# Differential attention: both scores of a tile ahead of its turns, and the low copy between the two exponentials

## What is computed

```python
def one(qblk):                                   # a block of 128 queries
    s = jnp.einsum('bqhsd,bkhsd->bhsqk', qblk, k).astype(jnp.float32) * scale
    p = jax.nn.softmax(s, axis=-1)
    a = p[:, :, 0] - lam * p[:, :, 1]
    return jnp.einsum('bhqk,bkhe->bqhe', a.astype(v.dtype), v)
```

## Time and profile before

| | us |
|---|---|
| median of 3 runs | 1749.78 (1749.14 to 1750.22) |
| profiled execution | 1748.26 |
| its span | 1746.5 |
| TensorE busy | 1702.2 (97%) |
| VectorE busy | 1210.1 (69%) |
| ScalarE busy | 809.1 (46%) |
| POOL busy | 806.2 (46%) |
| mean granted TensorE clock | 0.995 |

### The profile page before, as it was taken

How to read it: one execution, slowest core, us unless ns; L and a number is a source line. 1 busy time by engine, 2 the same in 40 slices (tenths; PEclk the granted TensorE clock), 3 DMA queues, 4 the chain that set the end, 5 groups by cost and what they waited for, 6 DMA issues and landing times. The chain is left out here.

```text
span 1746.5 us, 26024 instructions
## 1 busy us (share of the span) xinstructions
PE 1702.2 (97%) x9248; PEld 1439.5 (82%) x9248; DVE 1210.1 (69%) x1654; ACT 809.1 (46%) x1593; POOL 806.2 (46%) x579
## 2 busy tenths in 40 slices
PE   8999999999998999989999999899999999999998
PEld 7997888888877999879888878678888888878887
DVE  4438688789948999778733466866656655585767
ACT  3435333345637888657611246633333333354453
POOL 1308677776533899445422323455555555300000
PEclk9999999999999999999999999999999999999999
DMA  9333244335677665512054322132333232386734
GB/s 351 99 125 117 97 157 156 146 125 200 254 196 190 172 148 137 156 33 74 2 199 162 123 108 85 66 127 96 108 128 113 96 124 104 120 285 221 248 98 180
DMA packets 98571, 249.90 MB, mean 143 GB/s; under 512 B 12321, under 2 KB 26017, under 8 KB 98338
## 3 DMA queue, kind: packets, MB, share of 16 engines
q1 hardware_dynamic: 98466, 248.52, 42.6%
HBM read 183.07 MB, written 65.41 MB: 142 GB/s over the span
## 5 line engine op out<-in xcount | busy, mean ns | idle before, releaser
L766 POOL TENSOR_TENSOR ring<-raw_w,ring 128x512 fp32r<-128x512 f32 x120 | 187.1, 1579 | 137.3 <-ACT ring L637 137.3
L78 PE MATMUL psum<-h_hi,ring 128*128 128x512 f32 x400 | 155.9, 390 | 2.8 <-ACT z L683 2.0
L79 PE MATMUL psum<-h_lo,ring 128*128 128x512 f32 x400 | 155.6, 389 | 0.0
L80 PE MATMUL psum<-h_hi,ring 128*128 128x512 f32 x400 | 155.6, 389 | 0.0
L78 PE MATMUL psum<-u_slot 128*128 128x512 f32 x308 | 120.4, 391 | 1.3 <-DVE u_slot L2992 1.1
L80 PE MATMUL psum<-u_slot 128*128 128x512 f32 x308 | 120.1, 390 | 0.0
L79 PE MATMUL psum<-u_slot 128*128 128x512 f32 x308 | 119.9, 389 | 0.0
L637 ACT ACTIVATE ring<-raw_w 128x512 fp32r<-128x512 f32 x120 | 72.5, 625 | 102.0 <-DVE raw_w L927 39.3
L1418 DVE TENSOR_REDUCE mx<-psum 128x1 f32<-128x1280 f32 x64 | 95.1, 1487 | 6.7 <-PE psum L1304 6.0
L1351 ACT ACTIVATE e<-psum,neg_m 128x1280 f32<-128x1280 f32 x64 | 85.0, 1328 | 30.6 <-DVE neg_m L1419 30.6
L2591 POOL TENSOR_TENSOR cut_lo<-i_raw,cut_hi 128x512 fp32r<-128x512 f32 x44 | 66.8, 1519 | 59.3 <-ACT cut_hi L2446 59.3
(11 more groups left out here) (424 smaller groups left out, 5171.0 us busy)
## 6 DMA issues: line engine op xcount, KB each, us to landing
raw_w<-in_w_pairs SPq DMA_DIRECT2D x40, 512.0 KB, 4.9
qk_dram<-room SPq DMA_DIRECT2D x26, 512.0 KB, 3.6
room<-in_w_ada SPq DMA_DIRECT2D x24, 512.0 KB, 5.5
gates_dram<-ost SPq DMA_DIRECT2D x24, 512.0 KB, 3.1
b_g<-gates_dram SPq DMA_DIRECT2D x8, 1536.0 KB, 7.7
stage<-in_w_ff SPq DMA_DIRECT2D x22, 512.0 KB, 5.8
i_raw<-in_w_ff SPq DMA_DIRECT2D x22, 512.0 KB, 4.9
f_dram<-h SPq DMA_DIRECT2D x22, 512.0 KB, 3.3
```

The source lines that it names most:

```text
L78: pe.matmul(out, sh, mh, start=first, stop=False, skip_group_check=onto)
L79: pe.matmul(out, sh, ml, start=False, stop=False, skip_group_check=onto)
L80: return pe.matmul(out, sl, mh, start=False, stop=last, skip_group_check=onto)
L766: pool.tensor_tensor(w_lo[i], source(p, i), w_hi[i].bitcast(F32), ALU.subtract).then_inc(w_lo_ready, 1)
```

## The change

On TensorE the second scores of tile i move ahead of the wait for `a` and of the low turns; all ten turns then follow each other. On ScalarE the first exponential of tile i moves ahead of the copy of the low turns, which then stands between the two exponentials. Everything else stays: the same instructions with the same waits.

```diff
@@ -1321,12 +1321,10 @@
                 t = i - LAG_TURN
                 if i < TILES:
                     scores(i, 0)
+                    scores(i, 1)
                 if 0 <= t < TILES:
                     pe.wait_ge(a_ready, t + 3)
                     turn(t, i, "low")
-                if i < TILES:
-                    scores(i, 1)
-                if 0 <= t < TILES:
                     turn(t, i, "high")
                     bank = turn(t, i, "last")
                 elif t >= TILES:
@@ -1390,10 +1388,11 @@
             for s in range(2):
                 act.sem_inc(exp_done[s], 1)
             def step(i):
+                if i < TILES:
+                    exp(i, 0)
                 if LAG_TURN <= i < TILES + LAG_TURN:
                     copy_out(i, "low")
                 if i < TILES:
-                    exp(i, 0)
                     exp(i, 1)
                 if LAG_TURN <= i < TILES + LAG_TURN:
                     copy_out(i, "high")
```

## The result

The changed kernel takes 1803.55 us (median of four runs, 1800.86 to 1806.97), the kernel before beside it 1749.46 us. The ratio is 1.0309, with a 95% interval from 1.0296 to 1.0322: slower by 54 us. The profiled execution of the changed kernel took 1806.97 us, with a span of 1805.2 us.

A forecast was written before the change was run, and what follows sets the result against it. TensorE sets the pace, VectorE close behind. The change closes a six-term loop of 7.61 us a tile over 28 tiles, 52.6 us later, giving 1802.4 us; 4.5 for clock falls makes 1806 us, range 1797 to 1824.

The forecast's parts named there:

- The bound: Differential attention stage: TensorE sets the pace, busy 19.93 of 20 us, VectorE close behind at 18.59; ScalarE has room.
- The loop of 7.61 us: First scores, maximum, first exponential, low copy, last turns, products, next scores: six start-to-start distances, 7.61 us a tile.
- The wait of 1.8 us a tile: TensorE stands some 1.8 us in every tile before the last turns, until ScalarE has copied the low turns out.
- The sum for the stage: Differential attention: 28 tiles of 7.61 us, so the window stage begins at 758.4 instead of 705.83, 52.6 us later.
- The steps after the loop: Steps 32 to 34 of the stage have no exponential and keep their order, so they cost 0.
- The clock: TensorE's stops make its granted clock fall a few times: three falls, +4.5 us, bounds 0 and 14 falls (+21).
- The price of a fall: Each fall of TensorE's granted clock was estimated to cost 1.5 us.
- The rival with many falls: TensorE's clock falls in about every second tile or more: 14 falls of 1.5 us, 1823 us; chance 0.20.
- The rule of the Trainium skill: Short idles between matmul groups cycling through PSUM banks swing TensorE's clock; by it most tiles would have a slow stretch.
- The rival that works: Low copy done before TensorE reaches the last turns, 3.4 us after first scores; no loop, about 1744 us; chance 0.02.
- the saved switch: One switch from turns to scores on TensorE goes: at most 0.08 us a tile, 2.4 us in 30 tiles.

The follow-up runs named there:

- act_half: Kernel before the change with only ScalarE's half: low copy between the two exponentials, TensorE's order as before; 1802.16 us, ratio 1.029.
- low_after_both: Changed kernel with the low copy behind both exponentials instead of between them; 1903.6 us, ratio 1.087.
- both_filled: low_after_both with the four high turns of tiles 0 to 29 done five times over, sixteen transposes more a tile; 1850.96 us, ratio 1.0579.
- high_thrice: Changed kernel with the four high turns of tiles 0 to 29 done three times over, eight transposes more a tile; 1801.82 us, ratio 1.029.
- trim_three: trim_two with the last turns and products of the tiles in the loop put into the emptied bank 5; 1747.38 us, ratio 0.9984.
- trim_two: Changed kernel without the third piece (256 keys) of each tile's second scores, ring still of two banks; 1821.98 us, ratio 1.0412.
- pe_half: Kernel before the change with only TensorE's half: second scores ahead of all ten turns, ScalarE's order as before; 1757.77 us, ratio 1.0038.

## Why the prediction was right

- *The bound.* TensorE set the pace and ScalarE's low copy stood 1.34 us ahead of the first exponential, invisible in the list of waits. Right: act_half moves that copy alone and loses all of it.
- *The loop of 7.61 us.* Right to 0.01 us in each term (7.62 in the tile above); low_after_both and both_filled lengthen it by the term that was added, high_thrice shows that TensorE's turns are not in it, trim_three opens it.
- *The wait of 1.8 us a tile.* 47.3 us in 27 tiles in the list of 545 to 750 us: 1.89 us in the first, 1.73 to 1.76 in the others.
- *The sum for the stage.* Forecast 52.6 us; measured 54.4 us. Two traces have the same loop without a fall of the clock in it, act_half and high_thrice; their stages take 237.5 and 237.4 us, 52.8 us more than the 184.61 of before. So the loop was forecast to 0.2 us, and the other 1.5 us are one fall of the clock: tile 4's first scores come 8.73 us after tile 3's, tile 5's 8.25 us after tile 4's, together 1.76 more than twice 7.61, where the same two tiles of act_half take 0.22 more. The steps after the loop cost nothing, as said.
- *The clock.* The direction was right, the number of falls was guessed: three in the stage, one seen in this trace (the low stretch of 528 to 534 us in the earlier trace rows, before the loop closes, is in both kernels). It came behind the longest wait of the loop; the 28 waits of 1.73 to 1.76 us that followed left the clock at 1.00:

```profile
545.55 0.44 PE L1311 MATMUL psum<-ident,a 128*128 128x128 f32 x2 [1.89 <-ACT at L1356]
545.83 3.46 PE L1317 MATMUL psum<-val,at 128*128 128x128 f32 x20
```

```profile
547.00:550.00 3.00, 3.00 (x14) 2.81 (x14) 0.35 (x2) 0.92 (x4) 0.00 (x0) 0.50 1.10 366
550.00:560.00 10.00, 8.27 (x57) 7.38 (x56) 6.39 (x8) 4.94 (x13) 7.53 (x6) 0.98 0.42 167
550.00:755.00 205.00, 157.86 (x1131) 142.09 (x1130) 142.85 (x189) 124.98 (x271) 136.77 (x106) 1.00 0.46 123
```

  The forecast was 2.5 us above the median, and two falls too many, 3 us, are about that. That it came so near is partly luck: the four runs lie 6 us apart, and the profiled one has 4.3 us outside the stage for which the sum had no term. The price of a fall, 1.5 us, holds: trim_two's stage takes 257.3 us, 20 more than high_thrice's, and the products are slowed down in 13 of its tiles. The rival with many falls was closer than its trace made it look: trim_two, with 0.23 us more of waiting and as much less of work a tile, took 1821.98 us, where that rival had 1823.
- *The rule of the Trainium skill* ("TensorE: Matmul & The Clock Gate", section on psum-queue depth-cycling): the swing of the clock that it tells of is in low_after_both in nearly every tile and in trim_two in every second or third, not in the changed kernel. The pattern was the right one; the idles of the changed kernel, 1.74 us, were just short enough, where 1.97 us in trim_two were not.
- *The rival that works.* Its condition was named wrongly. I wrote that it decides at 3.4 us and that only the exponential stands in the way. pe_half has the exponential out of the way, and the copy still holds the last turns, by 0.25 us, since the low turns come later themselves. And its gain was priced too high: trim_three has the loop open, and of the saved switch, priced at 0.08 us a tile, some 0.02 are left. So the price of the change's benefit was wrong, with no effect on the sum, in which it was hidden.

## What to carry to other kernels

When an instruction is moved behind another in an in-order queue, list what the other one waits for and who waits for the moved one; if the second list leads back to the first, add up the start-to-start distances round the loop and compare the sum with the pace of now. A wait that doesn't show in a profile (here the one of the last turns for the low copy) is only a wait that is covered; a ring of two buffers that is used three times a tile has such a wait in each tile. And where TensorE is made to wait in every tile, look at how near the wait comes to one that drops its clock; work put into the wait, even useless work, can be worth more than the time it takes (53 us in both_filled; in high_thrice, where the clock was up already, nothing clear of noise).

## What the runs showed of the hardware

How sharply the clock answers to a wait that recurs. In tiles of 7.61 us, waits of 1.73 to 1.76 us never lowered it (28 in a row in the changed kernel, and 28 in act_half), one of 1.89 us did, and waits of 1.97 us did in every second or third tile (granted clock 0.91). A wait of 3.33 us a tile did so in nearly every tile (0.81); with 0.86 us in 7.61 or 1.6 us in 9.2 it stayed at 1.00. Between these kernels the length of the wait and the work in the tile changed together, so the runs don't tell which of the two decides. Twenty products at the low level took 4.48 us against 2.40, and since the loop goes through them, the falls in low_after_both cost 1.9 us a tile, 53 us in all: as much as the change that was studied.
